# Conv stage of a two-block kernel: the last chunk's shifted copies and tap products in token halves, its side sum joined before the taps, and pw1 weights stored slot by slot

## The chip, the cores and the metric

One core of a Trainium2 chip runs the whole program. The engines are TensorE (PE), VectorE (DVE), ScalarE (ACT), GpSimd (POOL) and SyncE (SP), which here only issues DMAs. The metric is the device time of one execution in microseconds, the median of several runs; smaller is better.

## The reference

Two transformer-like blocks of two layers each, 512 tokens by 1024 features, float32. Only the first layer's convolution module is touched:

```python
def conformer_conv(x, w_pw1, b_pw1, dw_w, dw_b, ln_g, ln_b, w_pw2, b_pw2):
    a = x @ w_pw1 + b_pw1
    u = a[..., :D_MODEL] * jax.nn.sigmoid(a[..., D_MODEL:])
    u = lax.conv_general_dilated(u, dw_w[:, None, :], window_strides=(1,),
            padding=[(CONV_WIDTH - 1, 0)], feature_group_count=D_MODEL) + dw_b
    u = jax.nn.silu(layer_norm(u, ln_g, ln_b))
    return u @ w_pw2 + b_pw2
...
```

`x` here is already rms-normed. The convolution is depthwise, causal, 31 taps wide. Attention, feed-forward layers and the second block follow and are not changed.

## The kernel before

Activations lie with features on the 128 partitions: chunk `c` of 8 holds 128 features by 512 tokens. Every large product is three TensorE passes (high by high, low by high, high by low part, lines L762 to L764) so that float32 accuracy is kept. The order on each engine is written out by hand, and semaphores tie the engines together. Weights come through a ring of four slots (`raw[j]`, in the trace `weight_raw`), are rounded to a high part by ACT (L3137, L2728) and the rest is computed by POOL (L2639, L2582).

**Start.** SP issues, in this order, small constants, input chunk 0, the first half of weight slot 0 (`half_slot(0, 0)`), chunks 1 and 2, the second half of slot 0, chunks 3 to 7, slot 1 in two halves. One half of a slot is 512 KB. ACT makes for each chunk `u_hi` (L3142) and a square (L3145), and between them it rounds the weight halves. DVE makes `u_lo` (L2241). PE's `high_passes` (L1403, L1404) take chunk after chunk, with filler products (`keep_warm`, L1365) between the first.

**Conv stage, chunk by chunk.** PE makes two tiles of chunk `c` (value and gate). DVE scales them by the inverse root mean square (`conv_scale`, L2282 and L2283), ACT takes the sigmoid (L2918), DVE multiplies both (`conv_gate`, L2292) into `conv_in[c % 3]`. Then the 31 taps of the chunk are spread over the engines:

- PE takes the first 12 or 16 (`PE_TAPS`). For these SP first copies `conv_in` inside the on-chip memory (`shift_copies`, L636): one copy for each quarter of 32 channels, each channel written four times, shifted by 0 to 3 tokens, so that one product of 128 rows does 4 taps of 32 channels. `pe_taps` (L1387) then multiplies with diagonal weights into `tap_bank(c)`. The four products of a group of taps go to four column quarters of the array.
- ACT and POOL take the last 7, of the last chunk the last 5 (`SIDE_TAPS`): ACT scales (L3183, L3194, L3188), POOL adds (L2619) and joins two partial sums (L2621) into `side_acc`.
- DVE takes those between (`conv_taps`, L2307 and L2309), 10 in the last chunk, and adds its two sums (L2318).

`conv_finish(c)` on DVE adds the PE bank (L2323) and then the side sum (L2325) to the chunk. It runs inside the taps of the chunk behind. `square_sum` (L2274) collects the squares that ACT makes of finished chunks (L3165). On DVE every linked instruction waits for the one before it (`d_chain`), and increments that stand by themselves come between.

**The last chunk (c = 7).** Nothing is behind it. PE sums chunks 0 to 6 over the partitions for the layer norm (`chunk_sums`, L939), waits for all four shifted copies, multiplies the 16 taps, adds the sum of squares (L949), waits for the finished chunk (L951, then its square, L953) and fills time (`keep_at_work`, L1360) until DVE and ACT have applied the layer norm. Then the product with `w_pw2` starts.

Of the kernel before, what the change touches and what calls it, by code (L numbers as in the profile page):

```python
# [22 lines left out]
P = 128  # L23
S = 512
# [10 lines left out]
OWN_FROM = min(PE_TAPS)  # L35
SIDE_TAPS = (7, 7, 7, 7, 7, 7, 7, 5)
PLE = 256
# [199 lines left out]
def build(nc, a, out):  # L237
    stages, landed_due, tiles_after, split_no, slot_width, hi_free = plan_slots()
    n_slots = len(slot_width)
    with ExitStack() as ctx:  # L240
# [12 lines left out]
        def sem(name):  # L253
            return ctx.enter_context(nc.semaphore(name))
# [120 lines left out]
        def quarter(j):  # L375
            return slice(j * QUARTER, (j + 1) * QUARTER)
# [5 lines left out]
        def tap_bank(c):  # L382

            return ps[:, 0] if c == DC - 1 else ps[:, 5 - c % 2]
# [46 lines left out]
        half_landed = [sem(f"half_landed{s}") for s in range(2)]  # L431
        conv_scaled = sem("conv_scaled")
        p_landed = sem("p_landed")
        bias_landed = [sem(f"bias_landed{s}") for s in range(2)]
# [113 lines left out]
        def _(sp):  # L548
# [4 lines left out]
            def half_slot(j, z):  # L553
                w = a["conv_w_pw1"].rearrange("(c p) n -> p c n", p=P)
                to = raw[j][:, z * DC * P:(z + 1) * DC * P].rearrange("p (c n) -> p c n", c=DC)
                transfer = sp.dma_start(to, w[:, :, z * D + j * P:z * D + (j + 1) * P])
                if z:
                    transfer.then_inc(landed[j], 32)
                else:
                    transfer.then_inc(half_landed[j], 16)  # L560
# [41 lines left out]
            def plain(w, at=0, kc=DC, width=256):  # L602
                return lambda st, slot: [(k_by(slot, kc, width), columns(w, st, lambda j: at + j * width, width))]

            def pair(wa, wb, at_a=0, at_b=0, kb=DC):
                def f(st, slot):
                    return [
                        (k_by(slot[:, 0:DC * P], DC, P), columns(wa, st, lambda j: at_a + j * P, P)),
                        (k_by(slot[:, DC * P:], kb, P), columns(wb, st, lambda j: at_b + j * P, P)),
                    ]  # L610
                return f
# [8 lines left out]

            load("pw1", pair(a["conv_w_pw1"], a["conv_w_pw1"], 0, D), only=2)
            sp.dma_start(con[:, CONSTS_FIRST:], a["consts"][:, CONSTS_FIRST:]).then_inc(con_landed, 16)
            sp.dma_start(early[0:BUCKETS, 0:HEADS], a["rel_bias"]).then_inc(inputs_landed, 16)
            sp.dma_start(early[0:BUCKETS + 1, 8:648], a["bucket_of"]).then_inc(inputs_landed, 16)
            load("pw1", pair(a["conv_w_pw1"], a["conv_w_pw1"], 0, D), only=3)

            def shift_copies(c):

                width = S + SHIFTS * (TAP_GROUPS[c] - 1)
                sp.wait_ge(conv_in_ready, c + 1)  # L630
                if c >= 2:
                    sp.wait_ge(pe_taps_done, c - 1)
                for j in range(SHIFTS):
                    channels = conv_in[c % 3][quarter(j), 0:width]
                    moved = bass.AP(channels.tensor, channels.offset, [[FC * S, QUARTER], [1, SHIFTS], [1, width]])
                    sp.dma_start(shifted_part(c, j, 0, width), moved).then_inc(shifts_landed[c % 2], 16)  # L636

            for c in range(DC):
                shift_copies(c)
                if c == 1:  # L640
                    sp.wait_ge(bias_sb, 1)
                    sp.dma_start(bias_rows, act[0:HEADS, 20 * S:20 * S + 640]).then_inc(bias_stored, 16)
                if c < DC - RING:
                    load("pw1", pair(a["conv_w_pw1"], a["conv_w_pw1"], 0, D), only=c + RING)
                else:
                    load("pw2", plain(a["conv_w_pw2"]), only=c - RING)
# [88 lines left out]
        def _(pe):  # L735
# [643 lines left out]
            def pe_taps(c):  # L1379
# [9 lines left out]
                mm.then_inc(pe_taps_done, 1)  # L1389

            def conv_slots():

# [72 lines left out]
                chunk_sums(0, DC - 1)  # L1465
                pe_taps(DC - 1)

# [159 lines left out]
        def _(dve):  # L1627
# [669 lines left out]
            def conv_taps(c):  # L2297
# [5 lines left out]
                for k, t in enumerate(taps):  # L2303
# [8 lines left out]
                    if k == 2 and c >= 2:  # L2312
                        square_sum(c - 2)
                if c == DC - 1:
                    square_sum(c - 1)
                if c < DC - 1:
                    conv_scale(c + 1)
                link(dve.tensor_tensor(y, own[len(taps) % 2], y, ALU.add))  # L2318

            def conv_finish(c):  # L2320

                dve.wait_ge(pe_taps_done, c + 1)
                link(dve.tensor_tensor(tap_bank(c), tap_bank(c), chunk(conv_out, c), ALU.add))  # L2323
                dve.wait_ge(side_added, side_adds[c + 1])
                link(dve.tensor_tensor(chunk(conv_out, c), tap_bank(c), side_acc[c % 2], ALU.add))  # L2325
                dve.sem_inc(side_used, 1)
                dve.sem_inc(pe_taps_used, 1)
                dve.sem_inc(h_ready, 1)
# [6 lines left out]
            for c in range(DC):  # L2335
                conv_taps(c)
                if c == 0:
                    bias_copies()
                    dve.wait_ge(con_landed, 16)
                if c < DC - 1:  # L2340
                    conv_gate(c + 1)
            conv_finish(DC - 1)
            link.begin(0)
# [1151 lines left out]
```

## Time and profile before

| what | value |
|---|---|
| median of 3 runs | 2496.99 us (2496.9 to 2497.02) |
| the profiled execution's own time | 2499.49 us |
| its span, first to last instruction | 2497.7 us |
| mean granted TensorE clock | 0.997 of full |
| PE busy | 2460.7 us, 99% of the span |
| PE weight loads busy | 1975.9 us, 79% |
| DVE, ACT, POOL busy | 54%, 40%, 44% |
| DMA | 282.09 MB, mean 113 GB/s |

Busy PE includes filler products and products at the halved clock. Times below are microseconds from the start of the span; the conv stage fills about the first 142.

### The profile page before, as it was taken

The page shows a single profiled execution, that of the slowest core. Times are in us where ns is not written, and L with a number is a line of the kernel's source. Part 1 is how long each engine was busy: PE and PEld are TensorE (multiplying, and loading weights), DVE is VectorE, ACT ScalarE, POOL GpSimd, SP SyncE. Part 2 cuts the span into 40 slices and gives each one's busy share as a digit, 9 for nine tenths or more (in the row PEclk, how much of TensorE's full clock was granted, in tenths as well). Part 3 has the DMA queues.
Part 4 walks back from the last instruction along what each step waited for, and adds up shares of the span by engine and source line. Part 5 has one row for each costly group of instructions (what it writes and reads, how often), then busy time and mean ns, then how long its engine had stood idle before and what let it go on. Part 6 is the DMA issues. An engine that isn't in the chain of part 4 may idle for free.

```text
span 2497.7 us, 31897 instructions
## 1 busy us (share of the span) xinstructions
PE 2460.7 (99%) x11826; PEld 1975.9 (79%) x11826; DVE 1351.0 (54%) x2136; ACT 988.2 (40%) x1386; POOL 1102.8 (44%) x560
## 2 busy tenths in 40 slices
PE   9999999999999999999999999999999999999998
PEld 6658888887777788888877878888888758888887
DVE  7856635634666465365338655551554465652553
ACT  6553222235555432223334254532344243532333
POOL 7844444444332344444443413544444313544443
PEclk9999999999999999999999999999999999999999
DMA  7535546533322365564353312324333122324322
GB/s 205 151 91 171 186 142 202 164 89 110 98 68 72 88 208 165 164 195 135 90 146 85 102 34 77 94 76 117 93 87 91 64 68 68 85 80 114 100 76 70
DMA packets 403610, 282.09 MB, mean 113 GB/s; under 512 B 10867, under 2 KB 382707, under 8 KB 403484
## 3 DMA queue, kind: packets, MB, share of 16 engines
q1 hardware_dynamic: 389660, 230.09, 32.6%
q10 hardware_dynamic: 13824, 50.34, 5.4%
q8 instruction: 78, 1.28, 0.2%
q14 instruction: 48, 0.39, 0.0%
HBM read 269.73 MB, written 2.12 MB: 109 GB/s over the span
## 4 chain that ended last, share of the span: by engine, by line
PE 92%; DVE 3%; ACT 3%; issue 1%; POOL 1%; DMA 0%; SPq 0%; DVEq 0%; ACTq 0%
PE ps L762 27%; PE ps L763 27%; PE ps L764 27%; PE ps L1387 1%; PE ps L1583 1%; PE ps L1149 1%; PE ps L1123 1%; PE ps L1262 1%; PE ps L1237 1%; PE ps L1111 1%; PE ps L1108 1%; DVE u_lo L1746 1%; PE ps L1525 0%; ACT weight_hi L2728 0%; PE ps L1251 0%
## 5 line engine op out<-in xcount | busy, mean ns | idle before, releaser
L2582 POOL TENSOR_TENSOR weight_lo<-weight_raw,weight_hi 128x1024 fp32r<-128x1024 f32 (+3 forms) x416 | 940.4, 2282 | 1316.2 <-ACT weight_hi L2728 1193.5
L764 PE MATMUL ps<-u_hi,weight_lo 128*128 128x512 f32 (+1 forms) x2424 | 916.1, 378 | 0.0
L762 PE MATMUL ps<-u_hi,weight_hi 128*128 128x512 f32 (+1 forms) x2216 | 866.1, 391 | 8.1 <-POOL weight_lo L2582 2.0
L763 PE MATMUL ps<-u_lo,weight_hi 128*128 128x512 f32 (+1 forms) x2216 | 855.8, 386 | 0.0
L2728 ACT ACTIVATE weight_hi<-weight_raw 128x2048 fp32r<-128x2048 f32 (+2 forms) x213 | 363.2, 1705 | 576.0 <-PE ps L764 544.1
L764 PEld LDWEIGHTS ps<-u_hi,weight_lo 128*128 128x128 f32 x2424 | 455.8, 188 | 85.6
L762 PEld LDWEIGHTS ps<-u_hi,weight_hi 128*128 128x128 f32 x2216 | 416.1, 188 | 114.2 <-issue 15.8
L763 PEld LDWEIGHTS ps<-u_lo,weight_hi 128*128 128x128 f32 x2216 | 416.3, 188 | 84.7 <-issue 2.9
L764 PE MATMUL ps<-act_hi,weight_lo 128*128 128x512 f32 (+1 forms) x748 | 281.5, 376 | 0.0
L762 PE MATMUL ps<-act_hi,weight_hi 128*128 128x512 f32 (+1 forms) x704 | 269.5, 383 | 0.0
L763 PE MATMUL ps<-act_lo,weight_hi 128*128 128x512 f32 (+1 forms) x704 | 269.2, 382 | 0.0
L1657 DVE TENSOR_TENSOR act_lo<-tmp,act_hi 128x512 f32 (+1 forms) x88 | 157.7, 1792 | 100.0 <-ACT act_hi L2736 100.0
L1982 DVE SCALAR_TENSOR_TENSOR tmp<-ps,par,tmp 128x510 f32<-128x510 f32 (+1 forms) x176 | 119.6, 742 | 153.4 <-ACT tmp L2978 153.4
L764 PEld LDWEIGHTS ps<-act_hi,weight_lo 128*128 128x128 f32 x748 | 140.5, 188 | 25.9
L763 PEld LDWEIGHTS ps<-act_lo,weight_hi 128*128 128x128 f32 x704 | 132.3, 188 | 25.8
L762 PEld LDWEIGHTS ps<-act_hi,weight_hi 128*128 128x128 f32 x704 | 132.3, 188 | 25.8
L1911 DVE SCALAR_TENSOR_TENSOR ps<-arena,small,ps 128x512 f32<-128x512 f32 x168 | 118.7, 752 | 34.8 <-DMA arena<-in_ada_w 28.0
L2978 ACT ACTIVATE tmp<-ps,par 128x512 f32<-128x512 f32 x88 | 59.6, 682 | 166.2 <-PE ps L764 166.2
L2927 ACT ACTIVATE tmp<-tmp 128x512 f32<-128x512 f32 x60 | 37.9, 632 | 199.4 <-DVE tmp L1942 139.7
L1861 DVE TENSOR_TENSOR ps<-ps,tmp 128x512 f32<-128x512 f32 x32 | 22.4, 700 | 130.3 <-PE ps L764 130.3
L2736 ACT ACTIVATE act_hi<-tmp 128x512 f32 (+1 forms) x88 | 55.1, 626 | 81.0 <-DVE tmp L1989 62.1
L1989 DVE TENSOR_TENSOR tmp<-tmp 128x512 f32<-128x512 f32 x44 | 55.3, 1257 | 34.1 <-ACT tmp L2983 34.1
(347 smaller groups left out, 2753.2 us busy)
## 6 DMA issues: line engine op xcount, KB each, us to landing
weight_raw<-in_ffn_w_up SPq DMA_DIRECT2D x132, 512.0 KB, 5.2
arena<-in_ada_w ACTq DMA_DIRECT2D x96, 512.0 KB, 5.7
weight_raw<-in_ffn_w_down SPq DMA_DIRECT2D x64, 704.0 KB, 4.7
weight_raw<-in_ffn_w_gate SPq DMA_DIRECT2D x44, 512.0 KB, 4.0
weight_raw<-in_ev_w_in SPq DMA_DIRECT2D x10, 1024.0 KB, 6.2
weight_raw<-in_conv_w_pw SPq DMA_DIRECT2D x16, 512.0 KB, 6.3
weight_raw<-in_ple_w_gate SPq DMA_DIRECT2D x16, 512.0 KB, 3.8
weight_raw<-in_attn_w_qkv SPq DMA_DIRECT2D x16, 512.0 KB, 5.4
```

The costliest lines, as they stand in the source:

```text
L762: pe.matmul(bank, w[0], x[0], start=start, stop=False)
L763: pe.matmul(bank, w[0], x[1], start=False, stop=False)
L764: return pe.matmul(bank, w[1], x[0], start=False, stop=stop)
L1657: dve.tensor_tensor(lo, t, hi.bitcast(F32), ALU.subtract).then_inc(x_ready, 1)
L1911: ada_link(dve.scalar_tensor_tensor(acc, row, by, acc, ALU.mult, ALU.add), 1 - z)
L1982: link(dve.scalar_tensor_tensor(y[:, back:], bank[:, 0:S - back], tap, y[:, back:], ALU.mult, ALU.add), spare)
L1989: dve.tensor_tensor(sq[par_], act_tmp[par_], rinv[par_], ALU.mult).then_inc(t_ready, 1)
L2582: low_part = pool.tensor_tensor(w_lo[r][:, cols], raw[r][:, cols], w_hi(k0 + j)[:, cols].bitcast(F32), ALU.subtract)
L2728: sc.activation(w_hi(slot)[:, 0:width], raw[slot % RING][:, 0:width], ACT.Copy).then_inc(w_rounded, 1)
L2736: sc.activation(dst, src, ACT.Copy).then_inc(hi_done, 1)
L2927: sc.activation(t, t, func).then_inc(act_done, 1)
L2978: sc.activation(y, bank, ACT.Copy, scale=tap).then_inc(act_done, 1)
```

## The change

1. The last chunk's shifted copies are cut into two token halves: four copies that hold what tokens 0 to 255 need (268 columns), then four with the other 256 columns, each half with a semaphore of its own. PE's taps of this chunk become `last_taps`, all taps of the first half, then all of the second.
2. One filler product stands on PE between the partition sums and these taps.
3. On DVE, `conv_gate(7)` moves ahead of the addition that ends chunk 6's taps; `square_sum(6)` moves up behind the seventh of the taps; one tap goes from DVE to ACT and POOL (`SIDE_TAPS` 5 to 6); the side sum is added to DVE's own sum before the wait for PE's taps, and only one addition is left behind that wait.
4. The host stores `conv_w_pw1` slot by slot, so that one partition's share of half a slot is one run of 4096 bytes, where it was 8 runs of 512 bytes. Bytes, number and order of these loads stay.

```diff
-SIDE_TAPS = (7, 7, 7, 7, 7, 7, 7, 5)
+SIDE_TAPS = (7, 7, 7, 7, 7, 7, 7, 6)
...
             def half_slot(j, z):
-                w = a["conv_w_pw1"].rearrange("(c p) n -> p c n", p=P)
-                to = raw[j][:, z * DC * P:(z + 1) * DC * P].rearrange("p (c n) -> p c n", c=DC)
-                transfer = sp.dma_start(to, w[:, :, z * D + j * P:z * D + (j + 1) * P])
+                cols = slice(z * DC * P, (z + 1) * DC * P)
+                transfer = sp.dma_start(raw[j][:, cols], a["conv_w_pw1"][j][:, cols])
...
-            load("pw1", pair(a["conv_w_pw1"], a["conv_w_pw1"], 0, D), only=2)
+            load("pw1", in_slots(a["conv_w_pw1"]), only=2)
...
-                for j in range(SHIFTS):
-                    channels = conv_in[c % 3][quarter(j), 0:width]
-                    moved = bass.AP(channels.tensor, channels.offset, [[FC * S, QUARTER], [1, SHIFTS], [1, width]])
-                    sp.dma_start(shifted_part(c, j, 0, width), moved).then_inc(shifts_landed[c % 2], 16)
+                middle = width - S // 2
+                for first, last in ((0, middle), (middle, width)) if c == DC - 1 else ((0, width),):
+                    for j in range(SHIFTS):
+                        channels = conv_in[c % 3][quarter(j), first:last]
+                        moved = bass.AP(channels.tensor, channels.offset, [[FC * S, QUARTER], [1, SHIFTS], [1, last - first]])
+                        done = shifts_landed[c % 2] if c < DC - 1 else last_shifts_landed[first > 0]
+                        sp.dma_start(shifted_part(c, j, first, last - first), moved).then_inc(done, 16)
...
+            def last_taps():
+
+                c = DC - 1
+                pe.wait_ge(diagonals_built, DC)
+                for z, cols in enumerate(HALVES):
+                    pe.wait_ge(last_shifts_landed[z], 16 * SHIFTS)
+                    for g in range(TAP_GROUPS[c]):
+                        for j in range(SHIFTS):
+                            mm = pe.matmul(tap_bank(c)[quarter(j), cols], tap_weights(c, g, j), shifted_part(c, j, SHIFTS * g + z * S // 2, S // 2),
+                                           start=g == 0, stop=g == TAP_GROUPS[c] - 1)
+                mm.then_inc(pe_taps_done, 1)
...
                 chunk_sums(0, DC - 1)
-                pe_taps(DC - 1)
+                keep_at_work(1, ps[:, 2])
+                last_taps()
...
-                if c == DC - 1:
-                    square_sum(c - 1)
+                    if k == 6 and c == DC - 1:
+                        square_sum(c - 1)
                 if c < DC - 1:
                     conv_scale(c + 1)
+                if c == DC - 2:
+                    conv_gate(c + 1)
                 link(dve.tensor_tensor(y, own[len(taps) % 2], y, ALU.add))
...
-            conv_finish(DC - 1)
+            y = chunk(conv_out, DC - 1)
+            dve.wait_ge(side_added, side_adds[DC])
+            link(dve.tensor_tensor(y, y, side_acc[(DC - 1) % 2], ALU.add))
+            dve.wait_ge(pe_taps_done, DC)
+            link(dve.tensor_tensor(y, tap_bank(DC - 1), y, ALU.add))
```

On DVE, from the scaling of chunk 7 to its end, before (line, operation, written<-read; `arena` is the finished sum, `act` holds `conv_in` and the side sum):

```order
L2283 TENSOR_TENSOR ps<-ps,tmp 128x512
L2318 TENSOR_TENSOR arena<-ps,arena 128x512 [waits d_chain]
L2292 SCALAR_TENSOR_TENSOR act<-ps,par,tmp 128x512 [waits pe_taps_done,side_ready,act_done,d_chain]
L2307 TENSOR_SCALAR ps<-act,par 128x512 [waits d_chain] x2
...
L2325 TENSOR_TENSOR arena<-ps,act 128x512 [waits side_added,d_chain]
L2309 SCALAR_TENSOR_TENSOR ps<-act,par,ps 128x512 [waits d_chain] x5
L2309 SCALAR_TENSOR_TENSOR arena<-act,par,ps 128x512 [waits d_chain]
L2274 TENSOR_TENSOR tmp<-ps,tmp 128x512 [waits squared,d_chain]
L2318 TENSOR_TENSOR arena<-ps,arena 128x512 [waits d_chain]
L2323 TENSOR_TENSOR ps<-ps,arena 128x512 [waits pe_taps_done,d_chain]
L2325 TENSOR_TENSOR arena<-ps,act 128x512 [waits side_added,d_chain]
```

and the same place after the change (L2312 is the gate, L2327 and L2329 the taps, L2294 `square_sum`, L2340 the addition of the two own sums, L2365 the side sum, L2367 the PE bank):

```order
L2303 TENSOR_TENSOR ps<-ps,tmp 128x512
L2312 SCALAR_TENSOR_TENSOR act<-ps,par,tmp 128x512 [waits pe_taps_done,side_ready,act_done,d_chain]
L2340 TENSOR_TENSOR arena<-ps,arena 128x512 [waits d_chain]
L2327 TENSOR_SCALAR ps<-act,par 128x512 [waits d_chain] x2
...
L2346 TENSOR_TENSOR arena<-ps,act 128x512 [waits side_added,d_chain]
L2329 SCALAR_TENSOR_TENSOR ps<-act,par,ps 128x512 [waits d_chain] x3
L2294 TENSOR_TENSOR tmp<-ps,tmp 128x512 [waits squared,d_chain]
L2329 SCALAR_TENSOR_TENSOR ps<-act,par,ps 128x512 [waits d_chain]
L2329 SCALAR_TENSOR_TENSOR arena<-act,par,ps 128x512 [waits d_chain]
L2340 TENSOR_TENSOR arena<-ps,arena 128x512 [waits d_chain]
L2365 TENSOR_TENSOR arena<-arena,act 128x512 [waits side_added,d_chain]
L2367 TENSOR_TENSOR arena<-ps,arena 128x512 [waits pe_taps_done,d_chain]
```

The gate and the final addition of chunk 6 changed places, one tap is gone, `square_sum` moved up by two taps, and the wait for `pe_taps_done` has one addition behind it instead of two. On PE, from the sums of chunks 0 to 6 to the last chunk's statistics, before:

```order
L939 MATMUL ps<-arena,con 128x512 [waits h_ready] x6
L1387 MATMUL ps<-act,arena 32x512 [waits diagonals_built,shifts_landed1]
L1387 MATMUL ps<-act,arena 32x512 x15
L949 MATMUL ps<-tmp,con 128x512 [waits sums_ready,pe_taps_used]
L951 MATMUL ps<-arena,con 128x512 [waits h_ready]
```

and after (L1367 is the filler product, L1406 the taps of `last_taps`):

```order
L946 MATMUL ps<-arena,con 128x512 [waits h_ready] x6
L1367 MATMUL ps<-con 128x512
L1406 MATMUL ps<-act,arena 32x256 [waits last_shifts_landed0,diagonals_built]
L1406 MATMUL ps<-act,arena 32x256 x15
L1406 MATMUL ps<-act,arena 32x256 [waits last_shifts_landed1]
L1406 MATMUL ps<-act,arena 32x256 x15
L956 MATMUL ps<-tmp,con 128x512 [waits sums_ready,pe_taps_used]
L958 MATMUL ps<-arena,con 128x512 [waits h_ready]
```

The sixteen tap products became twice sixteen of half the columns, each sixteen with a wait of its own, and the filler stands ahead of them.

## Rows read from the trace of the kernel before

**Rows 1.** Page, busy time of PE and the other engines over the span

```profile
PE 2460.7 (99%) x11826; PEld 1975.9 (79%) x11826; DVE 1351.0 (54%) x2136; ACT 988.2 (40%) x1386; POOL 1102.8 (44%) x560
```

**Rows 2.** Chain that ended last, 120 to 154: start, duration, what

```profile
124.91 0.55 SPq L636
...
127.49 5.38 DMA act<-act
...
132.91 5.38 PE ps L1387 x32
...
138.40 0.71 DVE ps L2323
...
139.13 0.70 DVE arena L2325
...
140.12 1.12 PE ps L951 x2
```

**Rows 3.** Timeline of PE: start, duration, instructions, [idle before <-releaser]

```profile
98.69 3.65 PE L1387 MATMUL ps<-act,arena 128*32 128x512 f32 x32
...
124.45 5.42 PE L939 MATMUL ps<-arena,con 128*128 128x512 f32 x12
130.17 1.12 PE L939 MATMUL ps<-arena,con 128*128 128x512 f32 x2 [0.30 <-DVEq L2328]
132.91 5.34 PE L1387 MATMUL ps<-act,arena 128*32 128x512 f32 x32 [1.62 <-DMA act<-act]
```

**Rows 4.** Busy by stretch: length, PE, PEld, DVE, ACT, POOL, clock, DMA share, GB/s

```profile
14.20:124.40 110.20, 110.20 (x569) 76.19 (x568) 91.27 (x139) 62.65 (x83) 98.92 (x62) 1.00 0.66 167
...
132.50:135.00 2.50, 2.09 (x12) 0.59 (x16) 2.43 (x4) 1.50 (x1) 0.85 (x1) 0.65 0.98 336
135.00:138.30 3.30, 3.30 (x25) 0.82 (x18) 0.69 (x1) 0.00 (x0) 3.30 (x1) 0.75 0.53 202
```

**Rows 5.** Timeline of DVE, chunk 7

```profile
123.98 0.75 DVE L2292 SCALAR_TENSOR_TENSOR act<-ps,par,tmp 128x512 f32<-128x512 f32 x1
124.98 1.41 DVE L2307 TENSOR_SCALAR ps<-act,par 128x512 f32<-128x512 f32 x2 [0.25 <-DVE act L2292]
...
130.20 3.39 DVE L2309 SCALAR_TENSOR_TENSOR ps<-act,par,ps 128x512 f32<-128x512 f32 x5 [0.34 <-DVE arena L2325]
...
135.21 0.69 DVE L2318 TENSOR_TENSOR arena<-ps,arena 128x512 f32<-128x512 f32 x1 [0.25 <-DVE tmp L2274]
```

**Rows 6.** Timeline of ACT and of POOL, chunk 7

```profile
122.64 0.72 ACT L2918 ACTIVATE tmp<-tmp,par 128x512 f32<-128x512 f32 x1 [1.74 <-DVE tmp L2282]
...
130.15 0.63 ACT L3165 ACTIVATE tmp<-arena 128x512 f32<-128x512 f32 x1 [1.96 <-DVEq L2328]
...
130.24 1.27 POOL L2621 TENSOR_TENSOR act<-act 128x512 f32<-128x512 f32 x1
```

**Rows 7.** DMA issues 124.8 to 125.2, the first shifted copy: size, us to landing

```profile
act<-act SPq DMA_DIRECT2D x1, 262.0 KB, 3.7
```

**Rows 8.** Timeline of ACT and of DVE at the start

```profile
6.48 1.06 ACT L3137 ACTIVATE weight_hi<-weight_raw 128x1024 fp32r<-128x1024 f32 x1 [0.58 <-DMA weight_raw<-in_conv_w_pw]
8.78 0.72 ACT L3142 ACTIVATE u_hi<-h,par 128x512 fp32r<-128x512 f32 x1 [1.25 <-DMA h<-in_x_t]
...
12.87 1.26 DVE L2241 SCALAR_TENSOR_TENSOR u_lo<-h,par,u_hi 128x512 fp32r<-128x512 f32 x1 [0.34 <-ACT u_hi L3142]
```

**Rows 9.** Busy by stretch, columns as in rows 4: what the DMA engines moved

```profile
4.00:5.50 1.50, 1.50 (x9) 1.50 (x8) 0.00 (x1) 0.85 (x2) 0.00 (x0) 1.00 1.10 319
9.50:11.50 2.00, 0.78 (x2) 0.69 (x3) 1.97 (x3) 1.99 (x5) 0.62 (x1) 0.71 1.06 389
...
50.00:52.00 2.00, 2.00 (x11) 1.65 (x10) 1.67 (x3) 0.63 (x1) 2.00 (x2) 1.00 1.01 290
126.00:129.00 3.00, 3.00 (x9) 1.32 (x8) 2.85 (x5) 2.18 (x4) 2.58 (x3) 1.00 0.90 129
```

**Rows 10.** Groups by line and form, PE, 256 columns: busy, mean ns

```profile
L980 PE MATMUL ps<-tmp,con 128*128 128x256 f32 x32 | 8.2, 379 | 0.0
```

More of the change, by code:

```diff
@@ L432, in build @@
         conv_scaled = sem("conv_scaled")
+        last_shifts_landed = [sem(f"last_shifts_landed{z}") for z in range(2)]
         p_landed = sem("p_landed")
@@ L603, in plain, with in_slots @@
                 return lambda st, slot: [(k_by(slot, kc, width), columns(w, st, lambda j: at + j * width, width))]
+            def in_slots(w):
+                return lambda st, slot: [(slot[:, z * DC * P:(z + 1) * DC * P], w[st.first][:, z * DC * P:(z + 1) * DC * P]) for z in range(2)]
             def pair(wa, wb, at_a=0, at_b=0, kb=DC):
@@ L624, in _ @@
             sp.dma_start(early[0:BUCKETS + 1, 8:648], a["bucket_of"]).then_inc(inputs_landed, 16)
-            load("pw1", pair(a["conv_w_pw1"], a["conv_w_pw1"], 0, D), only=3)
+            load("pw1", in_slots(a["conv_w_pw1"]), only=3)
             def shift_copies(c):
@@ L643, in _ @@
                 if c < DC - RING:
-                    load("pw1", pair(a["conv_w_pw1"], a["conv_w_pw1"], 0, D), only=c + RING)
+                    load("pw1", in_slots(a["conv_w_pw1"]), only=c + RING)
                 else:
@@ L2339, in _ @@
                     dve.wait_ge(con_landed, 16)
-                if c < DC - 1:
+                if c < DC - 2:
                     conv_gate(c + 1)
-            conv_finish(DC - 1)
+            y = chunk(conv_out, DC - 1)
[3 more added lines that the diff above has]
+            link(dve.tensor_tensor(y, tap_bank(DC - 1), y, ALU.add))
+            dve.sem_inc(pe_taps_used, 1)
+            dve.sem_inc(h_ready, 1)
             link.begin(0)
@@ L3475 @@
         "rel_bias": x["rel_bias"],
-        "conv_w_pw1": x["conv_w_pw1"][0], "conv_w_pw2": x["conv_w_pw2"][0],
+        "conv_w_pw1": x["conv_w_pw1"][0].reshape(DC, P, 2, DC, P).transpose(3, 1, 2, 0, 4).reshape(DC, P, SLOT), "conv_w_pw2": x["conv_w_pw2"][0],
         "attn_w_qkv": x["attn_w_qkv"][0], "attn_w_o": x["attn_w_o"][0],
```

## The prediction

> **What bounds the kernel now.** I read the page first: PE is busy 99% of the span [rows 1], so only work or waiting on PE's path counts. Then the chain that ended last between 120 and 154 us, because the change sits there: it leaves PE at the gate of chunk 7 and runs over SP's issues and the landing of the last shifted copy (132.87) to PE's taps, to two DVE additions, and back to PE at 140.12 [rows 2]. The timeline of PE shows what this costs it: an idle 0.30 us, then 1.62 us of waiting for the copies, and then 32 tap instructions that take 5.34 us where the same 32 took 3.65 us in an earlier chunk [rows 3]. The stretches say why: the granted clock is 0.65 and 0.75 of full in the two stretches of these taps, so most of them ran at the lower of the two levels (1.2 instead of 2.4 GHz), after PE had been mostly idle; in all 110.2 us between 14.2 and 124.4 PE is busy without a gap at the full clock [rows 4]. So two places have time to give: the tail of this stage, and the start before 14.2. Between them PE is solid, and a shift at the start moves the tail with it.
>
> **The gate, and the copies' start.** The sigmoid for the gate ends at 122.64 + 0.72 = 123.36 [rows 6], when DVE has just finished scaling the value tile. With 0.11 us from one engine's end to the next one's start (taps end 138.29, addition starts 138.40 [rows 2]) the gate can start at 123.47 instead of 123.98: the copies issue 0.51 us earlier, at 124.40. The addition that it overtakes pays: after the gate DVE waits 0.25 us [rows 5], so it starts at 124.22 + 0.25 = 124.47, and with 0.73 us from one chained addition to the next (138.40 to 139.13) the taps start at 125.20 instead of 124.98, 0.22 later.
>
> **DVE to its end.** The row of five taps then starts at 130.42. A tap takes (3.39 - 0.75)/4 = 0.66 us [rows 5]. Three taps to 132.40, `square_sum` 0.69 + 0.25 wait to 133.34, two taps (one fewer than before) of which the last starts at 134.00; the sum of the own parts at 134.77, the side sum at 135.50, and DVE is ready for PE's bank at 136.23. One addition: the chunk is whole at 136.92. Before, this was 139.13 + 0.69 = 139.82. The tail gives 2.90 us, if PE and the side sum are in time.
>
> **The side sum.** ACT's square of chunk 6 moves by 0.22 to 130.37 and ends at 131.0; the sixth side product behind it takes about 0.7, POOL's addition and the joining one 1.27 each [rows 6]: 134.3, with 1.2 us to spare before 135.50. The extra ACT and POOL time costs nothing here. It delays the next rounding and POOL's low half by some 0.7 us, work whose users come after the layer norm.
>
> **PE.** The sum over chunk 6 starts at 130.39 and takes two steps of 0.44 (12 take 5.42 [rows 3]); the filler takes another 0.87: 132.13. The taps keep their columns: a 256-column instruction lasts 379 ns against 592 for 512, so the halved part is half [rows 10, 3], and a half of the tokens costs 8 groups by 0.215 = 1.72 us at full clock. First half to 133.85, second to 135.57, some 0.2 until it is complete and 0.11 to DVE: 135.9. That is 0.35 us ahead of DVE's 136.23, so DVE is what sets the end. I take the full clock, since PE now idles only for about 0.5 us, around 130.2, and then has work without a gap, where the fall before followed an idle 1.62 us.
>
> **The copies in halves.** This is the unknown. A whole copy lands 3.7 us after its issue [rows 7], the fourth at 132.87: three steps of (132.87 - 128.61)/3 = 1.42 us. If the time goes by bytes, the first half has landed by 124.40 + 3.7 + 3 x 0.71 = 130.2, before PE asks at 132.13, and the second by 132.87 - 0.51 = 132.4, before PE asks at 133.85. If each copy costs 1.42 us whatever its size, the first is there at 132.4 and the second at 124.40 + 3.7 + 7 x 1.42 = 138.0. I take bytes: from 126 to 129, with nothing but these copies under way, the DMA engines are 0.90 busy [rows 9], so it is the moving and not the issuing that lasts, and eight issues fit into about 4.6 us at the 0.55 us of the first [rows 2]. There is room: the second half may land 1.8 us late before anything moves, 0.45 us for each of the four added copies. SP's later loads, held back by the added issues, are not asked for before the layer norm is done.
>
> **The start.** ACT begins the rounding of the first weight half at 6.48 and then idles 1.25 us until input chunk 1 has landed, 8.78; from there it goes without a wait to the operand that releases DVE at 12.87, and that releases PE's solid part at 14.2 [rows 8]. That chunk is queued behind the first weight half. In stretches full of 512-byte pieces the engines moved 319 and 290 GB/s, in one of 2048-byte pieces 389 [rows 9]. 512 KB, 524,288 bytes, take 1.64 to 1.81 us at the first and 1.35 us at the second: 0.29 to 0.46 us. The bounds are 0 and about 1.5 us: ACT cannot use more than its idle 1.25 plus what the weights themselves gain. I take 0.3. The weight half behind it gains as much again, so chunk 3, due later, is not what comes last next.
>
> The Trainium skill (page "DMA: Bandwidth & Descriptors", section "Specifications") puts the smallest transfer for line rate at 512 bytes, which would make this part worth nothing; rows 9 show a difference of a fifth. By the rule the forecast would be 2494.1 instead of 2493.8.
>
> **Sum.** Tail 2.90 and start 0.3: 3.2 us. On the profiled execution's 2499.49 us that is 2496.3; it ran 2.5 us above the median of the runs, and on the median, 2496.99, the forecast is 2493.8 us. It is 0.13%: what a measurement here can tell from no change is 0.2%, 5.0 us, so the class is "same".
>
> **Rivals.**
> *Each added copy costs as a whole one* (the opposite side). For it: a busy DMA share of 0.90 moves only 129 GB/s there, a third of the 389 of the input chunks [rows 9], so something other than bytes may set the pace, and SP's issues slow from 0.55 us for the first to a mean of (127.49 - 124.91)/3 = 0.86 [rows 2]. Against: what is slow are the pieces under way, and each becomes half as long. Second half at 138.0; PE has then been idle since 133.9, and its half of the taps at the low clock costs 5.34/2 = 2.67: whole at 138.0 + 2.67 + 0.1 + 0.7 = 141.5, that is 1.7 later than before, less 0.3 from the start: 2498.4. It loses against before from about 1.06 us for each added copy: second half at 136.6, whole chunk at 140.1.
> The Trainium skill (same page, "Rules for kernel authors") says to coalesce many small transfers into one large one, and speaks of mostly overhead below 64 KB; these halves have 128 KB and more, and no row here has a copy of that size.
> *The clock falls all the same.* For it: PE idles at 129.9 and again at 130.2, and the fall came some time after the idle stretch. The taps from 132.13 take 5.4 instead of 3.4: PE's part is done at 137.9, the chunk at 138.6, tail 1.2: 2495.5.
> *The start gives its bound.* Chunk 1 landed 2.3 us after the weight half ahead of it, far more than its 256 KB need; if the small pieces kept one DMA engine behind, the whole idle 1.25 goes: 2.9 + 1.5 = 4.4 us, 2492.6.
> *PE or DVE finds another 0.5 to 1 us,* such as halved tap products with more than half the cost: 256 columns come with 64 products and 64 weight loads where there were 32 each. At 0.3 us a group in place of 0.215 the taps end 1.4 later, the chunk 1.0 later: 2494.8.
>
> **Chances.** Forecast (gain 2.4 to 3.6 us) 0.52; start at its bound 0.12; costlier tap products 0.08; clock falls 0.08; copies costlier than their bytes, from 0.45 us each on, 0.15, a third of it beyond 1.06; anything not listed 0.05. The range for 8 in 10 goes from the start's bound to the middle of the costly copies: 2492.4 to 2496.6. Faster than 0.2% needs 5.0 us, more than all bounds of gain together (4.4): 0.05. Slower than 0.2% needs more than the worst rival: 0.02. The rest is same, 0.93.
>
> **What the changed profile would show.** The timeline of DVE: the gate at about 123.2, L2365 near 135.2 and L2367 near 135.9 (all 0.3 earlier by the start); its wait for PE's taps short or none. PE: L1406 in one piece of some 3.6 us right behind the filler, the granted clock at 1.00 in all stretches from 125 to 145, and L958 at 136.9. The copies: the second four landed by about 132.4. ACT at the start: L3142 of chunk 1 at 8.5. I am wrong if PE waits for the second half (copies), if L1406 at 1.00 takes over 4.5 us (products), if the clock shows 0.5 (clock), or if ACT's chunk 1 stands at 8.78 or well before 8.2 (start).

## The result, and the profile after

The changed kernel takes 2501.58 us (median of 19, 2500.19 to 2503.18) against 2497.02 us (median of 19, 2496.55 to 2498.75): 4.6 us slower, ratio 1.0017 with a 95% interval of 1.001 to 1.0024. The forecast was 2493.8 with a range up to 2496.6. The sign was wrong, and the time lies outside the range; only the class "same", a change under 0.2%, came out. The profiled execution took 2501.38 us with a span of 2499.6.

The page's busy times hardly move. DVE has one instruction less than before and is 4.6 us busier, PE has only 0.9 us more [rows 1]:

```profile
PE 2461.6 (98%) x11860; PEld 1978.2 (79%) x11860; DVE 1355.6 (54%) x2135; ACT 988.5 (40%) x1387; POOL 1103.4 (44%) x561
```

The chain that ended last, where [rows 2] went over the copies and PE's taps (start, duration, what):

```profile
134.39 0.70 DVE arena L2340
135.12 4.56 DVE arena L2365
139.70 0.70 DVE arena L2367
...
140.60 2.08 PE ps L958 x2
142.68 1.51 PE ps L960 x2
```

Neither a copy nor a tap product is on it. One addition, the side sum L2365, is there for 4.56 us. The timeline of PE, for [rows 3]:

```profile
124.09 5.42 PE L946 MATMUL ps<-arena,con 128*128 128x512 f32 x12
130.01 1.12 PE L946 MATMUL ps<-arena,con 128*128 128x512 f32 x2 [0.50 <-DVEq L2349]
130.97 1.02 PE L1367 MATMUL ps<-con 128*128 128x512 f32 x2
131.92 3.67 PE L1406 MATMUL ps<-act,arena 128*32 128x256 f32 x64
135.52 1.12 PE L956 MATMUL ps<-tmp,con 128*128 128x512 f32 x2
140.60 2.08 PE L958 MATMUL ps<-arena,con 128*128 128x512 f32 x2 [3.96 <-DVEq L2369]
142.47 1.70 PE L960 MATMUL ps<-tmp,con 128*128 128x512 f32 x2
```

The taps run in one piece right behind the filler and take 3.67 us, the 3.6 that was forecast. Then PE idles 3.96 us. The timeline of DVE, for [rows 5], with the gate at the top, and behind it that of POOL:

```profile
123.10 0.75 DVE L2312 SCALAR_TENSOR_TENSOR act<-ps,par,tmp 128x512 f32<-128x512 f32 x1 [0.24 <-DVE ps L2303]
124.09 0.69 DVE L2340 TENSOR_TENSOR arena<-ps,arena 128x512 f32<-128x512 f32 x1 [0.24 <-DVE act L2312]
...
134.39 0.69 DVE L2340 TENSOR_TENSOR arena<-ps,arena 128x512 f32<-128x512 f32 x1
135.12 4.55 DVE L2365 TENSOR_TENSOR arena<-arena,act 128x512 f32<-128x512 f32 x1
139.70 0.69 DVE L2367 TENSOR_TENSOR arena<-ps,arena 128x512 f32<-128x512 f32 x1
144.29 0.70 DVE L1697 SCALAR_TENSOR_TENSOR ps<-ps,tmp 128x512 f32<-128x512 f32 x1 [3.90 <-PE ps L960]
```

```profile
132.67 1.30 POOL L2648 TENSOR_TENSOR act<-act 128x512 f32<-128x512 f32 x1
134.60 4.51 POOL L2609 TENSOR_TENSOR weight_lo<-weight_raw,weight_hi 128x2048 fp32r<-128x2048 f32 x1 [0.63 <-ACT weight_hi L2755]
```

L2365 starts at 135.12, as forecast (135.2), and the side sum had been there since 133.97. Every other two-tile addition of DVE (TENSOR_TENSOR) from the gate to L2367 reads one operand from PSUM (`ps` behind the arrow) and takes 0.68 or 0.69 us; L2365 reads `arena` and `act`, both in SBUF. POOL began L2609 at 134.60 and ends it at 139.11; L2365 ends at 139.67.

The stretches of the tail, for [rows 4] (columns as there): the clock holds through the taps and falls after the idle time, so the two statistics products take 2.08 and 1.70 us instead of 1.12 and 1.02.

```profile
132.00:135.50 3.50, 3.50 (x64) 1.89 (x64) 3.19 (x6) 2.45 (x2) 2.79 (x3) 1.00 0.96 345
135.50:140.50 5.00, 1.14 (x6) 0.30 (x2) 4.86 (x2) 0.00 (x0) 3.61 (x1) 0.99 0.01 2
140.50:144.00 3.50, 3.40 (x4) 1.51 (x5) 0.00 (x0) 1.71 (x3) 0.13 (x1) 0.52 0.00 0
```

And the copies, for [rows 7] (KB each, median us from issue to landing): halves land sooner than whole ones (the first whole one took 3.7, the four of them 5.0 in the median), and PE never waits for them.

```profile
act<-act SPq DMA_DIRECT2D x4, 134.0 KB, 2.8
act<-act SPq DMA_DIRECT2D x4, 128.0 KB, 2.7
```

**A yardstick for the runs.** Two lengths are read from each profile: when PE's sums over the chunks start, and the *tail*, from there to the sum over the finished chunk (L951 before, L958 after). Before, that is 124.45 and 140.12 - 124.45 = 15.67 [rows 2, 3]; after, 124.09 and 140.60 - 124.09 = 16.51. So in these two profiles the start gained 0.36 us and the tail lost 0.84; the slow clock behind it (140.60 to 144.29 is 3.69 us, before 140.12 to 142.23 was 2.11) lost 1.58 more. That makes 2.1 us, and the spans differ by 1.9. The medians differ by 4.6. The other 2.7 us are a question of their own: what was special about the profiled execution of before? Its kernel's times come in two clusters; of 27 in one group of runs, 15 lie from 2496.72 to 2497.21 and 12 from 2498.19 to 2499.04.

### The profile page after: what moved, and what is told of

It reads as the page before. It is cut to its first block, busy times and chain, and to the rows that moved or that the text cites. A ratio compares the mean times of both kernels' runs of the same rounds, so it can differ in the third digit from the quotient of the medians.

```text
span 2499.6 us, 31970 instructions
## 1 busy us (share of the span) xinstructions
PE 2461.6 (98%) x11860; PEld 1978.2 (79%) x11860; DVE 1355.6 (54%) x2135; ACT 988.5 (40%) x1387; POOL 1103.4 (44%) x561
## 4 chain that ended last, share of the span: by engine, by line
PE 91%; DVE 4%; ACT 3%; issue 1%; POOL 1%; DMA 0%; DVEq 0%; SPq 0%; ACTq 0%
PE ps L769 27%; PE ps L770 27%; PE ps L771 27%; PE ps L1603 1%; PE ps L1156 1%; PE ps L1130 1%; PE ps L1394 1%; PE ps L1269 1%; PE ps L1118 1%; PE ps L1115 1%; PE ps L1244 1%; DVE u_lo L1766 1%; PE ps L1545 0%; ACT weight_hi L2755 0%; PE ps L1258 0%
## 5 line engine op out<-in xcount | busy, mean ns | idle before, releaser
L2609 POOL TENSOR_TENSOR weight_lo<-weight_raw,weight_hi 128x1024 fp32r<-128x1024 f32 (+3 forms) x416 | 939.1, 2279 | 1316.4 <-ACT weight_hi L2755 1193.9
```

The lines of the kernel that those rows point to most:

```text
L2609: low_part = pool.tensor_tensor(w_lo[r][:, cols], raw[r][:, cols], w_hi(k0 + j)[:, cols].bitcast(F32), ALU.subtract)
```

## The experiments

Theory A: L2365 waits for POOL, because both of its operands are in SBUF (the on-chip memory of the tiles called `arena`, `act` and `tmp`; `ps` is PSUM, the memory that PE writes), and the late chunk, PE's idle time and the fall of the clock all follow from that. Theory B: the length comes from the halved copies, from their traffic, or from the late side sum. Ten variants were run, and the kernel before profiled once more, in three groups on three chips, each beside the kernel before. Its medians there were 2497.25 (beside the PSUM operand, the early addition alone, the weights alone and the filler alone), 2498.14 (beside the idle POOL, the old storage and the whole copies) and 2497.17 (beside the last three variants). These medians shift with the share of the upper cluster, and the interval of every ratio to before includes 1 or, for the early addition alone, begins there. Differences of some tenths of a us between variants therefore count only where the profiles show them too.

### The side sum with one operand in PSUM, and the early addition alone

```diff
-                link(dve.tensor_tensor(y, own[len(taps) % 2], y, ALU.add))
+                link(dve.tensor_tensor(own[len(taps) % 2] if c == DC - 1 else y, own[len(taps) % 2], y, ALU.add))
...
-            link(dve.tensor_tensor(y, y, side_acc[(DC - 1) % 2], ALU.add))
+            link(dve.tensor_tensor(y, ps[:, 3], side_acc[(DC - 1) % 2], ALU.add))
```

> The changed kernel with one thing altered: the sum of DVE's own parts of chunk 7 stays in its PSUM bank, so that the addition of the side sum reads one operand from PSUM, where in the changed kernel both are in SBUF and it took 4.55 us (135.12 to 139.67) while POOL's L2609 ran from 134.60 to 139.11. Theory A (that addition, with both operands in SBUF, is held until POOL's running instruction ends): the addition takes 0.7 us, the chunk is whole near 136.5, PE idles about 1 us instead of 3.96, its clock does not fall, span about 2494 (5 to 6 us under the changed kernel's 2499.6), time about 2496 and below. Rival B (the addition waits for the side sum or is slow for another reason than its operands): still about 4.5 us, time as the changed kernel, 2501.5.

Measured: 2496.19 us (2495.75 to 2497.03, 11 runs), ratio to before 0.9995 (0.9986 to 1.0004), and 5.4 us less than the changed kernel. DVE, then PE, then POOL:

```profile
135.21 0.69 DVE L2365 TENSOR_TENSOR arena<-ps,act 128x512 f32<-128x512 f32 x1
135.94 0.69 DVE L2367 TENSOR_TENSOR arena<-ps,arena 128x512 f32<-128x512 f32 x1
138.94 0.70 DVE L1697 SCALAR_TENSOR_TENSOR ps<-ps,tmp 128x512 f32<-128x512 f32 x1 [2.31 <-PE ps L960]
```

```profile
124.18 5.42 PE L946 MATMUL ps<-arena,con 128*128 128x512 f32 x12
...
132.01 3.66 PE L1406 MATMUL ps<-act,arena 128*32 128x256 f32 x64
135.60 1.13 PE L956 MATMUL ps<-tmp,con 128*128 128x512 f32 x2
136.84 1.12 PE L958 MATMUL ps<-arena,con 128*128 128x512 f32 x2
```

```profile
134.69 4.54 POOL L2609 TENSOR_TENSOR weight_lo<-weight_raw,weight_hi 128x2048 fp32r<-128x2048 f32 x1 [0.63 <-ACT weight_hi L2755]
```

POOL works as long and at the same place, the copies and everything else are as in the changed kernel, and the addition takes 0.69 us. PE's idle 3.96 us and the slow clock are gone with it: the tail is 12.66 us.

The reverse, the kernel before with nothing but this addition moved ahead of the wait, both operands in SBUF:

```diff
-            conv_finish(DC - 1)
+            y = chunk(conv_out, DC - 1)
+            dve.wait_ge(side_added, side_adds[DC])
+            link(dve.tensor_tensor(y, y, side_acc[(DC - 1) % 2], ALU.add))
+            dve.wait_ge(pe_taps_done, DC)
+            link(dve.tensor_tensor(y, tap_bank(DC - 1), y, ALU.add))
```

> The kernel before with only the early joining of the side sum (both operands in SBUF, ahead of the wait for PE's taps), 5 side taps, copies and taps whole, weights as before. Theory A: the addition starts near 135.9 and ends about 0.6 us after POOL's low half (138.69), at 139.3; the final one ends at 140.0, about as before in the profiled execution (span 2497.7 to 2498.2). In unprofiled runs, where I suppose PE's taps often run at the full clock and end 1.9 us sooner than in the profile, it loses: 1.5 to 3 us slower than before, 2498.5 to 2500. Rival B (early join is a gain of one addition, as predicted): 0.7 us faster than before.

Measured: 2499.27 us (2498.88 to 2501.57, 11 runs), ratio 1.0009 (1.0 to 1.0018).

```profile
136.16 3.30 DVE L2344 TENSOR_TENSOR arena<-arena,act 128x512 f32<-128x512 f32 x1
139.50 0.69 DVE L2346 TENSOR_TENSOR arena<-ps,arena 128x512 f32<-128x512 f32 x1
```

```profile
134.37 4.55 POOL L2588 TENSOR_TENSOR weight_lo<-weight_raw,weight_hi 128x2048 fp32r<-128x2048 f32 x1 [2.63 <-ACT weight_hi L2734]
```

The addition starts 1.04 us later than in the changed kernel, beside a POOL instruction that ends 0.19 us sooner, and is 1.25 us shorter. It ends 0.54 us after POOL, where L2365 ended 0.56 after. So it does not take a fixed 4.5 us; it lasts until POOL is done and some 0.55 us more, a little less than its usual 0.69.

### The same two operands with POOL idle

```diff
-            low_halves("pw2", 1, 2)
             centre_conv()
-            low_halves("pw2", 2, 4)
+            low_halves("pw2", 1, 4)
```

> The changed kernel, with POOL's computation of the low half of w_pw2's slot 1 (L2609, 134.60 to 139.11 in the changed kernel) moved behind POOL's centring of the conv chunks. Both operands of the side sum L2365 stay on chip in the same memory as before. If the addition lasts 4.55 us because POOL is at work beside it, it now starts near 135.1 and lasts 0.7 to 0.8, PE's L958 starts at 136.8 to 136.9 without the idle 3.96 us, and the clock stays at 1.00; the time is then that of the kernel with the PSUM operand, 2496.2, plus what the late low half costs the product with w_pw2 (0 to 4.5 us, since its POOL work of 4.5 us is now the last thing before that product). If it lasts long because of its own operands alone, or of a DMA, it stays at 4.5 us beside an idle POOL and the time is 2501.6 or more.

Measured: 2496.02 us (2495.76 to 2497.64, 10 runs), ratio 0.9994 (0.9985 to 1.0003). DVE, then POOL:

```profile
134.88 0.69 DVE L2340 TENSOR_TENSOR arena<-ps,arena 128x512 f32<-128x512 f32 x1
135.61 0.69 DVE L2365 TENSOR_TENSOR arena<-arena,act 128x512 f32<-128x512 f32 x1
136.33 0.69 DVE L2367 TENSOR_TENSOR arena<-ps,arena 128x512 f32<-128x512 f32 x1
```

```profile
133.15 1.30 POOL L2648 TENSOR_TENSOR act<-act 128x512 f32<-128x512 f32 x1
139.62 4.96 POOL L2619 TENSOR_TENSOR arena<-arena,tmp 128x512 f32<-128x512 f32 x4 [5.17 <-ACT tmp L2833]
```

The very instruction of the changed kernel, with both operands in SBUF, takes 0.69 us while POOL idles. The late low half costs nothing that the time shows. So both conditions are needed, a running POOL instruction (here one that itself reads two tiles of SBUF) and no operand in PSUM, and theory B is out: copies, traffic and the side sum are as in the changed kernel.

### The parts at the start: weights slot by slot, and the filler

The kernel before with nothing but the new storage of `conv_w_pw1` (`half_slot`, `in_slots` and the host array, as in the change):

```diff
...
-                transfer = sp.dma_start(to, w[:, :, z * D + j * P:z * D + (j + 1) * P])
...
+                transfer = sp.dma_start(raw[j][:, cols], a["conv_w_pw1"][j][:, cols])
...
```

> The kernel before with only the pw1 weights stored slot by slot. The changed kernel's profile has the conv stage's partition sums 0.36 us earlier (124.09 for 124.45). If that is all: 0.3 to 0.4 us faster, 2496.6. Rival: the landing of the first weight half, 0.68 later in the changed profile (7.14 for 6.46), costs in unprofiled runs what the profile does not show: same or slower by up to 1 us.

Measured: 2497.83 us (2497.57 to 2500.66, 11 runs), ratio 1.0004 (0.9995 to 1.0013). The tail has 13.95 us, with the taps at 3.64, and the sums start at 124.61, no earlier than before. Next the filler alone, one line on PE:

```diff
+                keep_at_work(1, ps[:, 2])
                 pe_taps(DC - 1)
```

> The kernel before with only the one filler product between the partition sums and the last chunk's taps. Theory C (whether the clock falls for these taps differs between the profiled execution, 2499.49, and most unprofiled ones, 2497.0): the profiled span falls by about 1.9 to 2495.8, the median of the timed runs stays within 0.3 us of before. Rival D (the clock falls in every execution, as in the profile): the timed median falls by about 1.9 too, to 2495.1.

Measured: 2498.16 us (2496.56 to 2499.57, 11 runs), ratio 1.0 (0.9991 to 1.0009), spread over both clusters. The 1.9 us fall of the median, which would mean a low clock in every execution, did not come; for the rest it settles nothing about the filler. Its profile shows one thing: a time of 2498.44 with a tail of 14.01 and taps of 3.64 at full clock, because its sums started only at 124.96.

The storage once more, now undone in the kernel of the first experiment, so that only the weights differ:

```diff
-                cols = slice(z * DC * P, (z + 1) * DC * P)
-                transfer = sp.dma_start(raw[j][:, cols], a["conv_w_pw1"][j][:, cols])
+                w = a["conv_w_pw1"].rearrange("(c p) n -> p c n", p=P)
+                to = raw[j][:, z * DC * P:(z + 1) * DC * P].rearrange("p (c n) -> p c n", c=DC)
+                transfer = sp.dma_start(to, w[:, :, z * D + j * P:z * D + (j + 1) * P])
```

> The changed kernel with the PSUM operand in the side sum (2496.19 us), and the w_pw1 weights stored and loaded as before, in 512-byte runs. If the slot-by-slot storage gives 0.3 us at the start, as I forecast, this is 0.3 slower, 2496.5 us, with PE's sums over the chunks at 124.45 instead of 124.18. If it gives nothing or costs (the single edit was 0.6 us above before's median, and its first half slot landed 0.68 later in the changed kernel), this is 2495.6 to 2496.2 and the fastest version so far.

Measured: 2495.46 us (2495.06 to 2497.27, 11 runs), ratio 0.9992 (0.9983 to 1.0001), 0.73 us less than the first experiment, though that ran on another chip; the kernel with POOL idle (2496.02), which ran on the same chip with the new storage and a tail of 12.65, is 0.56 slower. The tail is unchanged at 12.66, and the sums start at 123.37 instead of 124.18. It has the lowest median of this study. ACT at the start, first this kernel, then the changed one (first rounding of weights and the operand of input chunk 1, for [rows 8]):

```profile
6.69 1.06 ACT L3165 ACTIVATE weight_hi<-weight_raw 128x1024 fp32r<-128x1024 f32 x1 [0.84 <-DMA weight_raw<-in_conv_w_pw]
7.65 0.71 ACT L3170 ACTIVATE u_hi<-h,par 128x512 fp32r<-128x512 f32 x1
```

```profile
7.17 1.06 ACT L3164 ACTIVATE weight_hi<-weight_raw 128x1024 fp32r<-128x1024 f32 x1 [1.51 <-DMA weight_raw<-in_conv_w_pw]
8.13 0.71 ACT L3169 ACTIVATE u_hi<-h,par 128x512 fp32r<-128x512 f32 x1
```

And the stretches while this weight half is on its way and a little later, in the same order:

```profile
4.00:6.00 2.00, 2.00 (x11) 2.00 (x11) 0.56 (x1) 1.24 (x2) 0.00 (x0) 1.00 1.05 304
8.00:10.00 2.00, 2.00 (x7) 1.68 (x8) 1.61 (x2) 2.00 (x5) 2.00 (x2) 1.00 1.12 360
```

```profile
4.00:6.00 2.00, 2.00 (x11) 2.00 (x11) 0.75 (x2) 1.24 (x2) 0.00 (x0) 1.00 0.95 231
8.00:10.00 2.00, 1.17 (x6) 0.90 (x6) 1.13 (x1) 2.00 (x5) 1.70 (x2) 1.00 1.02 401
```

The long runs do move more from 8 to 10 us, 401 against 360 GB/s; but from 4 to 6 us they move 231 against 304, and the first weights, the ones that ACT waits for, land later: ACT begins with them at 7.17 to 7.41 in all five profiles with the new storage, and at 6.31 to 6.73 in all eight with the old one. Chunk 1, which I meant to bring forward, was not waited for with the new storage. With the old one ACT did not wait for it in four profiles, waited 0.26 us in one, and 0.54, 1.23 and 1.25 us in three; the last is the profile that I had [rows 8]. Those three are also the ones with a late start: PE's sums begin at 124.96, 124.67 and 124.45 there, at 123.05 to 123.83 in the other five, and at 124.09 to 124.97 in all five with the new storage. So the new storage did take away the wait for chunk 1, which only some executions have; but the weights came later with it, and the start was late in all five.

### The halves, and what is left without them

The kernel of the first experiment with copies and taps whole again:

```diff
-                for first, last in ((0, middle), (middle, width)) if c == DC - 1 else ((0, width),):
+                for first, last in ((0, width),):
...
-                last_taps()
+                pe_taps(DC - 1)
```

> The changed kernel with the PSUM operand in the side sum (2496.19 us), and the last chunk's copies and taps whole again. The fourth whole copy should land at 132.87 - 0.36 - 0.5, about 132.0, where the first half is there at 128.87; PE's sums and the filler end at 132.0. If the halves matter little, the taps start at 132.0 to 132.3 and the time is 2496.2 to 2496.5. If a whole copy is held up on SP's queue as before, the taps start at 132.6 or later, PE idles 0.6 us and the time is 2496.8 or more. Should the taps fall to the half clock, it is 1.7 us more.

Measured: 2496.66 us (2496.3 to 2498.53, 11 runs), ratio 0.9996 (0.9987 to 1.0005). The taps start 132.90 - 124.97 = 7.93 us after the first sum, with halves 7.83, and the tail is 12.66 us in both. The 0.47 us between the medians is not in the tail; the two ran on different chips, and this profile's sums started late, at 124.97. The same with the old storage (the diff of the storage above, on top):

> The changed kernel with the PSUM operand in the side sum, the old storage of w_pw1, and whole copies and taps; what is left of the change is the order on DVE, the sixth side tap and the filler. I measure the tail from PE's first sum over the chunks to L958, the sum over the finished chunk: 14.05 us in the kernel before at full clock, 12.66 with and without the halves. If the halves give nothing this is 12.66 again and 2495.5 us, as with the halves (2495.46). If they give a little that the tail does not show, it is 2495.9 or more.

Measured: 2495.68 us (2495.33 to 2496.77, 11 runs), ratio 0.9993 (0.9984 to 1.0002), tail 12.65. That is not distinguishable from 2495.46, so the halves give nothing that the tail or the time shows. And with the filler taken out of this one as well:

```diff
-                keep_at_work(1, ps[:, 2])
                 pe_taps(DC - 1)
```

> The same without the filler product, so that PE idles about 1.3 us for the copies instead of 0.1. The end of the taps hangs on the copies either way, so at full clock the tail stays at 12.6 to 12.7 and the time at 2495.5. If the idle time makes the clock fall in the taps, as in the first profile of the kernel before, executions with taps of 5.3 us turn up and the median or the spread rises by up to 1.7 us; if the filler is without effect, the two kernels' times have the same spread.

Measured: 2495.92 us (2495.27 to 2497.27, 11 runs), ratio 0.9992 (0.9983 to 1.0001). PE idles 1.07 us for the copies, the taps still take 3.64 at full clock, and the tail is 12.79, since DVE now waits 0.18 for PE. What the filler is worth, if anything, stays open within these 0.24 us.

### The kernel before once more, and with a PSUM join only

No edit:

> The kernel before, profiled once more. Its first profile had the 32 tap products of the last chunk at the half clock (5.34 us), and a time of 2499.49 where the median is 2497.0; two kernels that leave these products as they are had them at full clock, 3.64. If the clock there is what parts the executions near 2497 from those near 2499, this one shows 3.64 with a span of about 2495.9 or 5.34 with one of about 2497.7, and nothing between; if not, the two do not go together.

Measured: 2496.81 us, one run, span 2494.7.

```profile
123.05 5.42 PE L939 MATMUL ps<-arena,con 128*128 128x512 f32 x12
...
131.59 3.64 PE L1387 MATMUL ps<-act,arena 128*32 128x512 f32 x32 [1.69 <-DMA act<-act]
...
137.10 1.13 PE L951 MATMUL ps<-arena,con 128*128 128x512 f32 x2 [0.81 <-DVEq L2328]
```

The same kernel as in [rows 3], with a tail of 14.05 instead of 15.67 and sums 1.40 earlier; together 3.02 us, and the spans differ by 3.0. Either alone seems to be enough for the upper cluster: the filler's 2498.44 had the late start and taps at full clock, and the next run has the reverse. PE idled no less ahead of the taps (1.69 against 1.62), and yet they ran at full clock. My expectation named only the taps' clock and a span of 2495.9; the start, which I had not named, is the other half.

Last, the kernel before with the early side sum, one operand in PSUM (`ps[:, 6]` here, as DVE has ten taps):

```diff
-                link(dve.tensor_tensor(y, own[len(taps) % 2], y, ALU.add))
+                link(dve.tensor_tensor(own[len(taps) % 2] if c == DC - 1 else y, own[len(taps) % 2], y, ALU.add))
...
-            conv_finish(DC - 1)
+            y = chunk(conv_out, DC - 1)
+            dve.wait_ge(side_added, side_adds[DC])
+            link(dve.tensor_tensor(y, ps[:, 6], side_acc[(DC - 1) % 2], ALU.add))
...
```

> The kernel before with one edit: the side sum is added ahead of the wait for PE's taps, with one operand in PSUM. It should take one addition, 0.72 us, off the tail: 13.3 instead of 14.05 at full clock, and 2496.2 to 2496.4 us against the fast cluster of before at 2496.9. With it and the full change's 12.66, the other 0.7 us is the earlier gate's. If the copies or the side sum are what ends last, it is 14.0 and 2496.9. If the new addition stalls as with two SBUF operands, it is 3.3 us long and the tail 15.7.

Measured: 2496.47 us (2496.26 to 2497.78, 11 runs), ratio 0.9995 (0.9986 to 1.0004). Its profiled execution was the slowest of the eleven, 2497.78, and has an early start and the taps at the lower clock:

```profile
123.21 5.42 PE L939 MATMUL ps<-arena,con 128*128 128x512 f32 x12
...
131.80 5.19 PE L1387 MATMUL ps<-act,arena 128*32 128x512 f32 x32 [1.75 <-DMA act<-act]
```

Its tail of 14.82 less the 5.19 - 3.64 = 1.55 us of slow taps is 13.27, the 13.3 expected: 0.8 of the 1.4 us that the tail can gain comes from this one moved addition. The other 0.6 comes from the rest of the change; how much of it is the earlier gate, the sixth side tap or the earlier `square_sum` was not taken apart.

## Why the prediction was wrong

**The step that failed.** "[...] the sum of the own parts at 134.77, the side sum at 135.50, and DVE is ready for PE's bank at 136.23." The addition was priced as one 0.73 us step like its neighbours, without asking where its operands lie and what runs beside it. It measured 4.55 us (3.86 more), with POOL's L2609 running from 134.60. Before, both additions of the last chunk behind PE's taps read `tap_bank`, in PSUM; the change turned one of them into an addition of two SBUF tiles, and moved it beside POOL. The cost that follows: PE idle 3.96 us, then 1.6 us at the low clock. 3.86 + 1.6 = 5.5; the first experiment gave 5.4 back. None of my rivals had this mechanism. The prediction did have POOL's low half in view, as work delayed by some 0.7 us "whose users come after the layer norm"; it asked who waits for that instruction, and not what runs beside it.

Behind this stands a rule of the Trainium skill that I had not weighed ("SBUF — State Buffer", section "SBUF: two separate sides"): VectorE and GpSimd share a pair of SBUF ports as an exclusive lock, which a VectorE operation with two SBUF inputs needs against a GpSimd operation that reads SBUF; whoever starts first keeps it for the whole instruction. The trace agrees: POOL started 0.52 us ahead, and L2365 ended 0.56 us after it.

The trace that I had also showed it, in rows that I did not ask for. The group of DVE that costs most in the kernel before has both operands in SBUF, and one of its instructions takes 1887 ns on average, while a neighbour of the same size with one operand in PSUM takes 691 (groups by line and form: busy us, mean ns):

```profile
L1657 DVE TENSOR_TENSOR act_lo<-tmp,act_hi 128x512 f32 x64 | 120.8, 1887 | 75.5 <-ACT act_hi L2736 75.5
...
L1942 DVE TENSOR_TENSOR tmp<-ps,tmp 128x512 f32<-128x512 f32 x44 | 30.4, 691 | 45.3 <-PE ps L764 45.3
```

Single instructions of that trace show the same thing as the experiments. L1657 from 1585.26 on takes 1.87 us and ends at 1587.13, 0.54 us after POOL's rounding (L2582, to 1586.59); the one at 1578.49, with POOL idle, takes 0.69. And L2241, with `h` and `u_hi` in SBUF, which I quoted in [rows 8] only for its start, takes 1.26 us at 12.87 beside a POOL instruction begun at 12.30, and 0.73 at 11.19, while POOL idles:

```profile
11.19 0.73 DVE L2241 SCALAR_TENSOR_TENSOR u_lo<-h,par,u_hi 128x512 fp32r<-128x512 f32 x1
12.30 2.98 POOL L2639 TENSOR_TENSOR weight_lo<-weight_raw,weight_hi 128x512 fp32r<-128x512 f32 x2 [2.18 <-ACT weight_hi L3137]
```

**The tail otherwise.** With that one addition repaired, every other step of the tail came out. I forecast the whole chunk at 12.47 us after the first sum (136.92 - 124.45); the first experiment has 12.45 (L2367 ends at 136.63). The gate came 0.52 earlier from the start of PE's sums (123.10 - 124.09 against 123.98 - 124.45), forecast 0.51. The copies came by their bytes or sooner (the last half, issued at 128.5, landed 2.9 us later, forecast 132.4), the taps took 3.67 us for 3.6, and the clock through the taps was 1.00. The halves were still worth nothing, since whole copies too let the taps start within 0.1 us of the same place. The rival of copies that cost as whole ones is refuted, and so are the costlier products. The clock did fall, but only behind PE's idle 3.96 us, and not in the taps as its rival had it.

**The basis of the sum.** "[...] it ran 2.5 us above the median of the runs, and on the median, 2496.99, the forecast is 2493.8 us": the gain was worked out on one execution and taken off the median of others. But what made that execution 2.5 us slow were the very things that the gain was to remove, taps at the low clock (1.6 us of tail) and a late start (sums at 124.45, where 123.05 was seen). An execution with the taps at full clock had a tail of 14.05, so the step from it to 12.66 was worth 1.4 us and not 2.9. Without the stall this alone would have made it 2495.6 before the start's share, near the 2495.46 and 2495.68 measured with the old weight storage.

**The start.** I forecast a gain of 0.3 us and found a loss of about 0.7 (2496.19 against 2495.46 across two chips, 0.56 on one). The idle time for chunk 1 belonged to some executions and not to others. And for the long runs I took the rate of 9.5 to 11.5 us, 389 GB/s [rows 9], where the first weights come in earlier: from 4 to 6 us the five profiles with the new storage moved 207 to 238 GB/s, the eight with the old one 294 to 336.

**The sum as it should have been.** 2497.0 - 1.4 (tail) + 0.7 (start) + 3.9 (addition) + 1.6 (clock) = 2501.8, against 2501.58 measured. All four terms were read after the result, so the agreement says that they cover the difference, and no more.

## What to carry to other kernels

Before an elementwise operation is moved, look up the memory of each operand and what POOL is doing at its new place; a group by form with a mean far above that of its size is the sign. If an intermediate sum can stay in PSUM until the last addition, as here at no cost that the runs show, the operation no longer waits for POOL. A gain that is read from one execution may be subtracted only from that execution: where it removes a slow clock or a late landing, take a second profile first and see whether they are there in it.

## What the runs showed of the hardware

- A DVE addition of 128x512 with both operands in SBUF, started while a POOL instruction that reads SBUF runs, ended 0.54 to 0.56 us after POOL's (4.55 and 3.30 us long); with one operand in PSUM beside the same POOL instruction, or with both in SBUF beside an idle POOL, it took 0.69.
- With weights in runs of 4096 bytes instead of 512, five profiles moved 401 to 415 GB/s from 8 to 10 us against 336 to 365 in eight, but 207 to 238 against 294 to 336 from 4 to 6 us, and ACT began with the first half slot 0.4 to 1.1 us later. Why the beginning is slower, no run here shows.
- Eight copies of 128 to 134 KB inside the on-chip memory landed 2.8 and 2.7 us after their issues (medians), where the first of four whole ones took 3.7 and the median of the four was 5.0.
- An idle 1.59 to 1.75 us of PE ahead of the taps was followed by the low clock in two profiles (5.34 and 5.19 us for 32 products) and by full clock in three (3.64 each), without order by the length of the idle time. What decides between them was not found.
